# RWKV time mix inputs, idle products and sparse attention's index scores, rewritten in one kernel of a whole two-layer model

## What is computed

```python
xx = jnp.pad(h, ((0, 0), (1, 0), (0, 0)))[:, :-1] - h            # shift difference
xm = h[None] + xx[None] * mix[:, None, None, :]                  # six mixes
xr, xw, xk, xv, xa, xg = xm[0], xm[1], xm[2], xm[3], xm[4], xm[5]
r = xr @ w_r;  k = xk @ w_k;  v = xv @ w_v                       # 1024 x 1024 each
w_log = -jax.nn.softplus(-(w0 + jnp.tanh(xw @ w1) @ w2)) - 0.5   # 1024 x 64, 64 x 1024: decays
a = jax.nn.sigmoid(a0 + (xa @ a1) @ a2)                          # 1024 x 64, 64 x 1024: rates
g = jax.nn.sigmoid(xg @ g1) @ g2                                 # 1024 x 160, 160 x 1024: gate
kk = k * k_k, each head of 64 divided by its length
k = k * (1.0 + (a - 1.0) * k_a)
y = wkv7_scan(r, exp(-exp(w_log)), k, v, -kk, kk * a)            # the recurrence, 16 heads
bonus = (sum(r * k * r_k) per head) * v;  return ((norm(y) + bonus) * g) @ w_o

# attention, for each block of 128 queries: 8 index heads score all keys, 64 keys are kept
rel = relu(einsum("bqhd,bkhd->bqhk", qi, ki));  score = einsum("bqh,bqhk->bqk", wi, rel)
_, idx = lax.top_k(score, topk)
logits = einsum(qg, kg) * scale;  softmax over the kept keys;  o = p @ vg      # 16 heads, 4 key heads
```

## Time and profile before

| | us |
|---|---|
| median of 3 runs | 2140.13 |
| the three runs | 2139.15, 2140.13, 2152.64 |
| the profiled execution | 2132.1 |
| its span, first to last instruction | 2130.3 |

### The profile page before, as it was taken

How to read it: one execution, slowest core, us unless ns; L and a number is a source line. 1 busy time by engine, 2 the same in 40 slices (tenths; PEclk the granted TensorE clock), 3 DMA queues, 4 the chain that set the end, 5 groups by cost and what they waited for, 6 DMA issues and landing times.

```text
span 2130.3 us, 43769 instructions
## 1 busy us (share of the span) xinstructions
PE 2013.0 (94%) x17458; PEld 1896.2 (89%) x17458; DVE 1055.2 (50%) x1623; ACT 922.0 (43%) x1590; POOL 1279.0 (60%) x528
## 2 busy tenths in 40 slices
PE   7999798999999999999978999999999988999997
PEld 7999587778799999999865999989998877898997
DVE  5770766665668716860465577021263244324431
ACT  4333453111343344343436543444446555656552
POOL 6887253000278877786630688967656554677885
PEclk9999899999999999999989999999999999999999
DMA  6444132000244454454320355544354332343552
GB/s 267 170 175 175 73 138 80 3 3 2 80 158 177 166 174 157 177 180 174 125 74 1 139 177 185 192 176 158 125 210 142 139 112 90 135 179 140 191 185 77
DMA packets 40919, 291.96 MB, mean 137 GB/s; under 512 B 4432, under 2 KB 5712, under 8 KB 5712
## 3 DMA queue, kind: packets, MB, share of 16 engines
q1 hardware_dynamic: 40640, 288.92, 38.0%
q10 hardware_dynamic: 144, 1.05, 0.1%
HBM read 288.90 MB, written 1.05 MB: 136 GB/s over the span
## 4 chain that ended last, share of the span: by engine, by line
PE 31%; issue 28%; POOLq 19%; POOL 18%; ACT 1%; DVE 1%; DMA 0%; DVEq 0%; SPq 0%; ACTq 0%
POOLq L1894 18%; POOL w_low L1890 18%; PE ps L587 9%; PE ps L595 9%; PE ps L591 9%; PE ps L1283 1%; PE ps L1271 1%; PE ps L1261 1%; PE ps L699 0%; POOLq L1889 0%; DMA X<-x_in 0%; ACT units L1796 0%; ACT units L1348 0%; POOLq L1906 0%; DVE units L1916 0%
## 5 line engine op out<-in xcount | busy, mean ns | idle before, releaser
L1890 POOL TENSOR_TENSOR w_low<-wring,w_high 128x1024 fp32r<-128x1024 f32 x524 | 1278.8, 2455 | 830.1 <-ACT w_high L1348 800.8
L587 PE MATMUL ps<-in_high,w_high 128*128 128x256 f32 (+1 forms) x2856 | 829.1, 290 | 33.7 <-DVE in_low L1916 12.9
L595 PE MATMUL ps<-in_high,w_low 128*128 128x256 f32 (+1 forms) x2856 | 819.4, 287 | 0.0
L591 PE MATMUL ps<-in_low,w_high 128*128 128x256 f32 (+1 forms) x2856 | 819.3, 287 | 0.0
L1348 ACT ACTIVATE w_high<-wring 128x1024 fp32r<-128x1024 f32 x524 | 542.3, 1055 | 286.4 <-PE ps L587 281.8
L587 PEld LDWEIGHTS ps<-in_high,w_high 128*128 128x128 f32 x2856 | 545.1, 191 | 42.9 <-issue 37.3
L595 PEld LDWEIGHTS ps<-in_high,w_low 128*128 128x128 f32 x2856 | 545.7, 191 | 0.0
L591 PEld LDWEIGHTS ps<-in_low,w_high 128*128 128x128 f32 x2856 | 544.6, 191 | 0.5
L587 PE MATMUL ps<-hid_high,w_high 128*128 128x272 f32 (+1 forms) x880 | 254.9, 290 | 0.0
L595 PE MATMUL ps<-hid_high,w_low 128*128 128x272 f32 (+1 forms) x880 | 250.7, 285 | 0.0
L591 PE MATMUL ps<-hid_low,w_high 128*128 128x272 f32 (+1 forms) x880 | 250.5, 285 | 0.0
(11 more groups left out here) (331 smaller groups left out, 2580.6 us busy)
## 6 DMA issues: line engine op xcount, KB each, us to landing
wring<-stream SPq DMA_DIRECT2D x271, 1024.0 KB, 4.8
con<-consts SPq DMA_DIRECT2D x1, 2199.0 KB, 16.0
X<-x_in SPq DMA_DIRECT2D x1, 1088.0 KB, 7.6
units<-decay ACTq DMA_DIRECT2D x1, 1024.0 KB, 4.8
out<-AL SPq DMA_DIRECT2D x1, 1024.0 KB, 4.7
par<-params SPq DMA_DIRECT2D x1, 187.0 KB, 4.9
con<-consts SPq DMA_DIRECT2D x1, 130.0 KB, 7.5
```

Source lines behind the costliest of these rows:

```text
L587: mm = pe.matmul(o, wh, high(k), start=(k == 0), stop=False)
L591: mm = pe.matmul(o, wh, low(k), start=False, stop=False)
L595: mm = pe.matmul(o, wl, high(k), start=False, stop=(k == kt - 1))
L1890: pool.tensor_tensor(w_low[:, (half + h) % SPLIT_RING, :], wring[:, slot, h * HALF * P:(h + 1) * HALF * P], w_high[:, (half + h) % SPLIT_R ...
```

## The change

There are three parts in one diff.

**Inputs of the time mix.** (a) rk_w1 and rk_a1 become one product. Since (H + m T2) W = H W + T2 (m W), TensorE multiplies H with the 64 columns of each matrix into the lower and upper half of one bank, and adds T2 times scaled weights, `rk_scaled`, that ScalarE makes before the norm by 16 copies of 128 x 64; the w and a mixes disappear. (b) rk_w2 and rk_a2 leave the stream; two DMAs of 64 rows at the start bring them into SBUF (`rk_second`), one ring load disappears, and their products are 8 pairs of matmuls with 64 rows each, on the upper and the lower half of the rows: two pairs before rk_k, the others one after each of its tiles. (c) rk_g1 goes from group 3 of the recurrence to the place behind the first product; in group 3 ScalarE copies its result. (d) The r mixes move from before rk_k into it, one for each tile, and the v mixes, their lows, reciprocal and logs change places in rk_r; both mixes are written to PSUM banks, and the lows read them there. (e) The spreads of kk go to yields 6 and 8, the bonus sums to 4 and 6, the exponent to tile 7, and the preparation of group 1 ahead of the second bonus product. Before the norm, three halves of rk_k's weights are split instead of two.

**Idle products.** Group 3's last level gets fill(7, 4) before two of its chunks, and attention loses the two fill(6, 4) of step m = 1.

**Attention.** Index scores of both blocks come at yields 9 to 13, ahead of the sums for the key norm, with `ds_score` cut out of `ds_select`; block 1's score has a tile of its own. The turned values are called at 15, 16 and 17. The queries are turned and roped by group of four heads, `ds_rope(g)`, groups 2 and 3 between the biased logits.

The core of the diff:

```diff
             load(3, 3)
+            for half in range(2):
+                sp.dma_start(rk_second[HD * half:HD * half + HD, :],
+                             stream[ASIDE_SLOT][0:HD, half * DT * P:(half + 1) * DT * P]
+                             ).then_inc(S["rk_second_loaded"], 16)
...
+            def rk_first_product():
+
+
+
+                at = [stage_number(name) for name in ("rk_w1", "rk_a1")]
+                tile = tiles_before[at[0]]
+                o = ps[:, BANK[tile], 0:T]
+                bank_free(tile)
+                for k in range(DT):
+                    for half in range(2):
+                        w = weight_tile(PLAN_STARTS[at[half]] + k)
+                        if half == 0:
+                            pe.wait_ge(S["rk_normed"], rk_normed(k))
+                        mm = pe.matmul(o[HD * half:HD * half + HD, :], w[:, 0:HD], H[:, k, :],
+                                       start=(k == 0), stop=False)
...
+                    pe.wait_ge(S["rk_normed"], rk_shifted(k))
+                    pe.wait_ge(S["rk_first_shifted"], k + 1)
+                    mm = pe.matmul(o, rk_scaled[:, k, :], T2[:, k, :], start=False, stop=(k == DT - 1))
+                mm.then_inc(S["linear_ready"], 2)
...
+            def rk_second_product(i):
...
+                for half in range(2):
+                    rows = slice(HD * half, HD * half + HD)
+                    pe.matmul(ps[:, (6 if i == 1 else 3) + half, 0:T], rk_second[rows, i * P:(i + 1) * P],
+                              rk_lora[rows, 0, :], start=True, stop=True).then_inc(S["rk_wa2_ready"], 1)
...
+            def rk_seconds():
+
+
+                for i in range(DT):
+                    rk_second_product(i)
+                    if i:
+                        yield i - 1
+
+            rk_first_product()
+            linear("rk_g1", lambda k: T1[:, k, :], before_k=lambda k: pe.wait_ge(S["rk_mixed_g"], k + 1))
+            beside(split_tiles("rk_k", lambda k: in_high[:, k, :], lambda k: in_low[:, k, :], T,
+                               lambda k: pe.wait_ge(S["rk_split"], k + 1)), rk_seconds())
...
-                    if 1 <= m <= 4:
+                    if 2 <= m <= 4:
                         fill(6, 4)
                     ds_values(*DSA_STEPS[m - 2])
                 if 1 <= m <= len(DSA_STEPS):
-                    if m <= 4:
+                    if 2 <= m <= 4:
                         fill(6, 4)
                     ds_turn(*DSA_STEPS[m - 1])
...
-            R, K, V, W, B, G = (A[:, 8 * i:8 * i + 8, :] for i in range(6))
+            R, K, V, W, B = (A[:, 8 * i:8 * i + 8, :] for i in range(5))
...
+                in_bank = lambda k: ps[:, rk_mix_bank(k), 0:T]
...
+                receptances = mixed_parts(1, "r", in_bank, r_high, r_low)
+                next(receptances)
                 for k in range(DT + 1):
...
+                    next(receptances)
                     dve.drain()
                     if k < DT:
+                        dve.wait_ge(S["rk_wa2_emptied"], 2 * k + 2)
                         dve.wait_ge(S["rk_kk_squared"], k + 1)
                         stt(K[:, k, :], B[:, k, :], -1.0, u, ALU.add, ALU.mult)
...
-                for k in range(DT):
-                    mix("v", mixed[:, k, :], k)
-                dve.drain()
+                for k, _ in enumerate(mixed_parts(2, "v", in_bank, in_high, in_low)):
+                    if k == 3:
+                        dve.wait_ge(S["rk_kk_summed"], 1)
...
+                dve.wait_ge(S["rk_kk_rooted"], 1)
+                dve.reciprocal(rms[0:16, 0, :], rms[0:16, 1, :]).then_inc(S["rk_kk_inv"], 1)
                 for c, (t0, C) in enumerate(CHUNKS):
                     ins = tt(W[:, :, t0:t0 + C], W[:, :, t0:t0 + C], tiles_of(rk_mid[:, c, :], DT, C), ALU.subtract)
...
+            def ds_rope(g):
...
+                tt(o, ps[:, 4 + g, :].rearrange("p (u t) -> p u t", u=2), tokens_of(const("sin")[:, TB], 2), ALU.mult)
+                stt(A[:, v, TB], A[:, v, TB], column("q_g"), tokens_of(const("cos")[:, TB], 2), ALU.mult, ALU.mult)
+                dve.drain()
+                tt(A[:, v, TB], A[:, v, TB], o, ALU.add).then_inc(S["ds_q_ready"], 1)
...
+                if m < 2:
+                    ds_rope(m + 2)
```

More of the change, by code:

```diff
@@ L5 @@
+import itertools
 from contextlib import ExitStack
@@ L67 @@
          "nsa_mg", "nsa_out", "mix_out")
-TIME_MIX = ("rk_w1", "rk_w2", "rk_a1", "rk_a2", "rk_k", "rk_r", "rk_v", "rk_g1", "rk_g2", "rk_o")
+TIME_MIX = ("rk_w1", "rk_a1", "rk_g1", "rk_k", "rk_r", "rk_v", "rk_g2", "rk_o")
+ASIDE = ("rk_w2", "rk_a2")
 def device_order():
@@ L76, in device_order @@
         at = names.index(first)
+        taken = [*taken, *ASIDE] if first == "rk_r" else taken
         order[at:at + len(taken)] = [names.index(name) for name in taken]
-    return order
+    return [i for i in order if names[i] not in ASIDE] + [names.index(name) for name in ASIDE]
 ORDER = device_order()
@@ L443, in build @@
             dve_before.append(n_dve)
-            for i in range(nt):
+            for i in range(0 if name in ASIDE else nt):
                 if name == "ffn":
@@ L1550, in _ @@
             act.wait_ge(S["consts_loaded"], 16)
-            begin("rk_k")
+            number = PLAN_STARTS[stage_number("rk_w1")] // PER
+            act.wait_ge(S[f"slot{number % RING}_loaded"], 16 * (number // RING + 1))
+            for half, m in enumerate((1, 4)):
+                for k in range(DT):
+                    w = wring[:, number % RING, (half * DT + k) * P:(half * DT + k) * P + HD]
+                    copy(rk_scaled[:, k, HD * half:HD * half + HD], w, param("mix", m)[:, k:k + 1])
+            high_parts_to(half_at(PLAN_STARTS[stage_number("rk_k")]) + 3)
             norm(1, T, full)
-            linear("rk_w1", lambda i: rk_lora[:, 0, :], lambda i: ACT.Tanh)
-            linear("rk_w2", lambda i: A[:, 24 + i, :], lambda i: ACT.Sigmoid, param("w0"))
+            for k in range(DT):
+                act.wait_ge(S["rk_normed"], rk_normed(k))
+                copy(T2[:, k, 0:1], H[:, k, 0:1], -1.0).then_inc(S["rk_first_shifted"], 1)
             def finished(name, i):
```

284 lines of the change are left out of this document (149 added, 135 removed).

## The result

| | us |
|---|---|
| before: median of 4 runs (least, greatest) | 2141.3 (2139.2, 2152.6) |
| changed: median of 4 runs (least, greatest) | 2118.1 (2117.5, 2122.4) |
| ratio of the runs | 0.9883, 95% interval 0.9853 to 0.9913 |
| changed, profiled execution and its span | 2117.5, 2115.7 |

The change makes the kernel 1.2% faster; the interval of the ratio excludes 1. The forecast was 2112 with a range of 2097 to 2132.

The account below looks back on a forecast made before the run. It took TensorE, busy 94% of the span, as the bound. Inputs -15.2, recurrence -5 and attention -7.5 sum to -27.7 on 2132.1 us, 2104.4; plus 8.0 for the median, 2112, range 2097 to 2132.

Parts of the forecast that it names:

- Inputs, ahead of rk_k (-8.3 against -10.2): First products of the time mix: rk_k starts at 242.8 instead of 252.95, -10.2 us.
- Rival 4: First product and pairs: column and row halves do not run beside each other, 3.8 later and +4.5; 2120; chance 0.08.
- rk_k (+3.8 against -1): Stage rk_k with six pairs and r mixes added: 29 us instead of 30.05, -1, bounds -2.4 to +11.
- The 30.4: rk_k: eight tiles of 3.8 us if VectorE's locked operations and GpSimd's exclude each other.
- the 27.6: rk_k: 24.2 us of matmuls plus six pairs of 0.56, if TensorE bounds.
- Rival 1: VectorE and GpSimd exclude each other, VectorE bounds rk_k (+11) and rk_r (+8); 2136; chance 0.15.
- rk_r (-5.7 against -2): Stage rk_r: reciprocal wait of 3.0 and about 2 of half clock go, 3 given back: -2, bounds 0 to -6.
- rk_v (-0.7 against -2): Behind rk_v: preparing group 1 ahead of the second bonus product removes TensorE's whole 1.9 wait, -2.
- Recurrence (-6.1 against -5): Group 3: 8.9 us of rk_g1 leave, 2.9 put on new waits, about 1 of idle matmuls added: -5.
- Rival 2: Recurrence: the levels of group 3 do not shorten, gain 0; 2117; chance 0.10.
- Attention (about -5 in three of six traces, -2.5 in the changed kernel's own, against -7.5): Attention: earlier selection -8.9, split ropes -3.7, groups 2 and 3 +2.5, lower clock 2.6 back: -7.5.
- The +8.0 that I added for the median: Whole kernel: the profiled execution of 2132.1 is 8.0 us below the runs' median, so 2104.4 becomes 2112.

Follow-up runs that it names:

- joined: Changed kernel with rk_w1 and rk_a1 side by side as one 128-column weight tile, one matmul on H for both: 2116.1 us.
- mix_one_input: Changed kernel with the r mixes leaving H out, so one SBUF input instead of two (r is another value): 2112.8 us.
- mix_by_scan: Changed kernel with each r mix directly ahead of its tile's scan on VectorE, behind low part and gate: 2113.4 us.
- no_fill_g3: Changed kernel without the two calls of idle products in group 3's last level and the wait for masks ahead of them: 2117.8 us.
- attention_only: Kernel before with the attention part of the change alone: ratio to before 0.9965.
- fills_back: Changed kernel with the two calls of four idle products at attention's step m = 1 put back: 2119.4 us.
- ropes_later: Changed kernel with the ropes of query groups 2 and 3 moved behind the first weighting of probabilities: 2107.9 us.

## Why the prediction held, point by point

**Inputs, ahead of rk_k (-8.3 against -10.2).** The mechanism was right: TensorE started at 224.54, the clock was up at 228.6 at the latest, rk_g1 took 7.4. The term that was mis-sized is the tile: 1.27 us warm instead of 0.96. I priced the two halves together and the full matmul at 0.48 each; they cost 0.61 and 0.65, and joined shows that it is the halves. Rival 4, no overlap of the halves, is false as a mechanism, since the records of two halves lie beside each other; but by its price (3.8 us over eight tiles) a tile takes 1.44, and 1.27 is nearer to that than to 0.96. The pairs of row halves took the 0.56 that I had put (1.12 for the two from 243.52 on). The -8.3 has luck in it: four of the other traces with this product took 1.2 to 1.7 us more, as the clock rose later; the first product is longer than 12 us there, which was rival 4's sign, and 11.6 here. The Trainium skill's sentence on packing ("TensorE: Matmul & The Clock Gate", Part 3) says that tiles at other places of the array run at the same time, and the trace agrees; but the pair costs a third more than one full matmul here.

**rk_k (+3.8 against -1).** This is the step that failed, twice over. The 30.4 for a VectorE and a GpSimd that exclude each other left out that GpSimd gets in between mix and scan: one tile waits for two different w_low, the next for none, 8.9 us for the two (the scans at 263.12 and 271.99). And the 27.6 for a rk_k that TensorE bounds was too low: without any wait it takes 29.7 (mix_one_input, busy 29.70). So 29 could not have been reached even without the lock, and that mix_by_scan comes out at 30.34, next to my 30.4, is chance: there too TensorE is what fills the stage. Rival 1 named the lock, and its sign, mixes of 2 us and more, was there; its size, +11, was too large, and it did not become the bound of rk_r. mix_one_input (29.71) and mix_by_scan (30.34) against 33.85 show the lock as the cause, and the second that it is the order and not the work. The rule of the Trainium skill ("SBUF — State Buffer", Who interferes with whom) is borne out in both halves: two SBUF inputs wait (1347 ns), one does not (430 to 499 ns).

**rk_r (-5.7 against -2).** The 3.0 wait and the half clock behind it went; the 3 us that I gave back for reciprocal and logs did not come: TensorE is busy 32.8 of 33.0. It came out near the end of my bounds, -6.

**rk_v (-0.7 against -2).** The 1.9 wait is still there at L764. The preparation was not what it waited for. It waits for VectorE's product of the bonus and v for the last four tiles (`rk_bonus_read`), which ScalarE's copy of rk_v's last tile releases. That operation before, and now:

```profile
351.01 1.29 DVE L1916 TENSOR_TENSOR AL<-ps,AL 128x1088 f32<-128x1088 f32 x1 [8.73 <-ACT AL L1348]
```

```profile
340.10 1.29 DVE L2001 TENSOR_TENSOR AL<-ps,AL 128x1088 f32<-128x1088 f32 x1 [3.46 <-ACT AL L1420]
```

TensorE goes on at 352.40 and at 341.50, 0.1 us behind their ends.

**Recurrence (-6.1 against -5).** Of 8.9 us removed, 1.3 came back as idle products (no_fill_g3) and some 1.5 as short idle stretches. Rival 2 is false. What the table hides is that rk_g1 has only moved: its 7.4 us ahead of rk_k are as much as the levels gave up, and the idle products come on top. No run left rk_g1 where it was, so whether the move pays is open.

**Attention (about -5 in three of six traces, -2.5 in the changed kernel's own, against -7.5).** The first turned probabilities came 8.3 us earlier from at_in's start, instead of 10.1. The selection is what was mis-sized: `ds_k_ready` itself came 1.0 later (1069.20 against 1085.22, with the shift of 17.1), its start is 8.8 earlier instead of 9.9, and it took 11.7 instead of 10.6 us to the first rope, so that it ended 7.7 earlier where I had 8.9. That 8.8 lies next to my 8.9 is therefore no hit. The split ropes gave 3.5 (3.7), and those of groups 2 and 3 cost 2.9 (2.5). The waits of the turned values that went, 2.5 in all, shortened at_in, but behind it TensorE waits for VectorE anyway. Behind the first turned probabilities the low clock took 3.2 back in attention_only (56.6 us against 53.4 before) and 5.8 in the changed kernel (59.2), where I had 2.6. The size was near in the first; the reason, the missing idle products, is not shown: with them (fills_back) it was 56.5 too. ropes_later shows what still holds the first turned probabilities: the ropes of groups 2 and 3.

**The sum.** -22 us with -5.0 for attention and nothing for the token mixer's clock, -23.2 in the medians, -27.7 forecast. Errors of +4.8 (rk_k), +1.9 (first product), +2.5 (attention), +1.3 (rk_v), -3.7 (rk_r) and -1.1 (recurrence) make the 5.7 between them. That the total came within 6 us is partly luck: 10.5 us of error one way met 4.8 the other. The +8.0 that I added for the median was right, though I had given no reason: it is the luck of the one profiled execution of before.

## What to carry to other kernels

When work moves beside GpSimd, count the VectorE operations with two SBUF inputs and look where in the tile they stand: adjacent, they went through one gap of GpSimd here; apart, each met a GpSimd operation of its own. Before explaining a few microseconds by the edit, compare the same stage in several traces: here a stage without an edit moved by 5 us. A kernel whose own stages repeat within 0.1 us is best judged stage by stage, and the medians only confirm.

## What had not been expected of the hardware

- The length of a stretch at the lower clock differs between executions of the same instructions. At the changed kernel's first product the clock rose 3 to 4 us after the first matmul in three traces and 6 to 7 us after it in six (two of them with joined weights); at the gate behind the recurrence it was low for none or some 10 us; at one place of the token mixer for 3 or 10. TensorE does half as much in such a stretch (71 records against 130 in 14 us). Over all runs of before, 2133 to 2158 us, the mean clock goes from 0.979 in the fastest to 0.965 in the slowest. Times the span that is 31 us of lost clock, more than the 25 us between them, so the clock is enough to explain the spread.
- Two column halves of an fp32 matmul take 0.61 us, and the full matmul behind them takes 0.65, where full ones in an unbroken row take 0.46 each.
- Stages without such a stretch repeat within 0.02 us: rk_k took 33.84 to 33.86 in six traces, rk_r 33.00 to 33.01 in seven (33.11 in the two with the mix beside the scan), rk_v, up to the first score of group 1, 30.00 to 30.01 in nine.
